# Ring slots of the expert tables' chunks: spacing of 4224 bytes in place of 4096

## The chip, the core and the metric

One core of a Trainium2 chip runs the whole kernel. The time is the device time of one execution in microseconds. TensorE multiplies, ScalarE, VectorE and GpSimd compute beside it, and SyncE issues most of the DMAs. All of them read and write one on-chip memory of 128 partitions; an address below is a byte offset inside a partition.

## What is computed

A decoder layer over 256 tokens of width 1024, in float32:

```
h = x + concat(norm(moba_attention(q_m, k_m, v_m)), norm(stick_breaking(q_s, k_s, v_s))) @ w_out
xn = rms_norm(h, ffn_norm)
# PEER: for each token 8 heads choose 16 experts each, of 128 * 128
hid = gelu(xn . u_table[expert])
h = h + sum over the chosen experts of gate * hid * v_table[expert]
h = h + sigmoid(rms_norm(h, ple_norm) @ w_gate) * (p @ w_ple)
```

The expert part is done densely. The kernel multiplies all 16384 rows of `u_table` with all tokens, multiplies the result by the gates (zero where an expert wasn't chosen), and multiplies that with all of `v_table`. Each table is 64 MB, read as 128 chunks of 128 experts, 512 KB each.

## The kernel before

**Precision.** A float32 operand is split in two parts of the matmul's own format, `hi` (a rounded copy) and `lo` (the rest), and each product is three matmuls: hi x hi, hi x lo, lo x hi. `three` (L1203 on) issues them: its first argument of a pair is the weights (stationary), the second the moving operand. So the weights run `ah, ah, al` and the moving operand `bh, bl, bh`.

**The ring.** A chunk of a table goes to one of `RING = 4` slots. `t_raw` holds the loaded float32 chunk, `t_hi` its rounded copy (ScalarE, `table_hi`, L583), and `t_lo` the rest (GpSimd at L1178 in the first pass, VectorE at L910 in the second), written in place of `t_raw`. Both tiles are `[P, RING, D]` with D = 1024, so the slots of each lie 4096 bytes apart. SyncE reloads a slot when TensorE is done with the chunk in it (`hid_done`, `v_used`), and ScalarE and the engine of `t_lo` work `LEAD = 2` chunks ahead of TensorE.

**The first pass** (L1440 on, some 190 to 583 us). For each chunk `hidden(q)` issues 24 matmuls: eight column blocks of 128 of `t_hi`, `t_hi`, `t_lo` as weights, and `xt_hi`, `xt_lo`, `xt_hi` (128 x 256, the normalised tokens) as moving operand. The result goes through Gelu into `slots`. From chunk 40 on (`late_step`) three of four chunks are followed by four matmuls of `gates` (L1481, weights `hot_i`, moving `hot_j`, 256 columns), which build the gates of four tokens.

**The second pass** (`expert_sum`, L1510 on, some 583 to 933 us). For each chunk 12 matmuls: weights `g_hi`, `g_hi`, `g_lo` (128 tokens each), moving operand `t_hi`, `t_lo`, `t_hi` (512 columns). They accumulate in four PSUM banks over all chunks.

**The other large products** have `xt_hi`, `xt_hi`, `xt_lo` as weights and 512 or 256 columns of `w_hi`, `w_lo` (or `wg_hi`, `wg_lo`) as moving operand (`rows_group`, `projection`, the end at L1563), or the reverse in `columns_group` (L1234). `embedding` has `pt_hi`, `pt_lo` as weights and `wp_hi`, `wp_lo` as moving operand.

**The addresses.** All tiles are placed by hand. `sizes` gives, in this order, `h` (8192 bytes), `xt_hi` (8192), `gains` (128), `xt_lo` (8192), `cst` (2048), `qkg` (128), `stats` (768), and then `ZONE` begins, with the ring and what goes with it. `BIG` begins behind that zone, with `w_raw`, `w_hi`, `w_lo`, `slots` and, 98304 bytes on, the tiles at `UP`.

Of the kernel before, what the change touches and what calls it, by code (L numbers as in the profile page):

```python
# [36 lines left out]
TOPK = 16  # L37
PH = 8
# [5 lines left out]
WARM = 3  # L44
RING = 4
LEAD = 2
FIRST = 40
EXP_AT = 32
PICKS_AT = 36
# [22 lines left out]
def layer_program(nc, x, x_t, p_t, rel_bias, bucket_onehot, consts, qk_gain, w_in, w_out, w_query,  # L72
# [5 lines left out]
    with ctx:  # L78
# [5 lines left out]
            where[name] = at  # L84
            at += 4 * n
        ZONE = at
        BIG = ZONE + 4 * 13312
        assert BIG + 4 * P * SEQ <= nc.sbuf_usable_end

        def tile(name, shape, offset, dt=f32):  # L90
# [28 lines left out]
        o = UP  # L119
# [41 lines left out]
        diag = tile("diag", [P, SEQ], ZONE + 4 * 10752)  # L161
        rstd_row = tile("rstd_row", [P, SEQ], ZONE + 4 * 11008)

        t_raw = tile("t_raw", [P, RING, D], ZONE)
        t_lo = tile("t_lo", [P, RING, D], ZONE, f32r)
        hit = tile("hit", [P, PH, TOPK, TOPK], ZONE + 4 * 4096)
        hot_i = tile("hot_i", [P, 2, 4, P], ZONE + 4 * 4096, f32r)
        hot_j = tile("hot_j", [P, 2, 4, 2, P], ZONE + 4 * 5120, f32r)
        g_hi = tile("g_hi", [P, RING, SEQ], ZONE + 4 * 4096, f32r)
        g_lo = tile("g_lo", [P, RING, SEQ], ZONE + 4 * 5120, f32r)  # L170
        t_hi = tile("t_hi", [P, RING, D], ZONE + 4 * 7168, f32r)
        o = ZONE + 4 * 11264
        pick_t = tile("pick_t", [P, 3, SEQ], o); o += 4 * 768
        sk = tile("sk", [P, 2, N_KEYS], o); o += 4 * 256
        pick = tile("pick", [P, TT, 2, P], o); o += 4 * 512
        gate = tile("gate", [P, TT, PH, TOPK], o); o += 4 * 256
        ratio = tile("ratio", [P, SEQ], o); o += 4 * 256
        assert o <= BIG
        low = tile("low", [P, 2, 4, P], ZONE + 4 * 12032)
        gate_hi = tile("gate_hi", [P, SEQ], ZONE + 4 * 12032, f32r)  # L180
        gate_lo = tile("gate_lo", [P, SEQ], ZONE + 4 * 12288)

        pairs = [ctx.enter_context(nc.psum_tensor(f"pair{k}", [P, 4, 2, P], f32)) for k in range(2)]
        bank = [pairs[b // 2][:, 2 * (b % 2):2 * (b % 2) + 2, :, :].rearrange("p a b c -> p (a b c)")
# [115 lines left out]
        @block.sync  # L300
        def _(sp):
            for c in range(2):
                sp.dma_start(w_raw[:, 0, c, :], w_in[0, :, c, :]).then_inc(piece_loaded[c], 16)
            for b in range(1, 4):
                cols = slice(4 * DC + 2 * SEQ * b, 4 * DC + 2 * SEQ * (b + 1))
                sp.dma_start(xt_raw[:, 2 * b:2 * b + 2, :].rearrange("p a b -> p (a b)"), x_t[:, cols]
                             ).then_inc(xt_loaded[b], 16)
                sp.dma_start(w_raw[:, 0, 2 * b:2 * b + 2, :], w_in[0, :, 2 * b:2 * b + 2, :]
                             ).then_inc(piece_loaded[b + 1], 16)
            for b in range(4):  # L310
                sp.dma_start(w_raw[:, 1, 2 * b:2 * b + 2, :], w_in[1, :, 2 * b:2 * b + 2, :]
                             ).then_inc(quarter_loaded[b], 16)
# [12 lines left out]
            sp.wait_ge(*split(0))
            for k in range(2):
                m = slice(256 * k, 256 * (k + 1))
                sp.dma_start(w_raw[:, 0, :, m], w_in[2, :, :, m]).then_inc(half_loaded[k], 16)
            for n in range(3, N_GROUPS):
                load_group(n)  # L330
                if n == 3:
                    sp.wait_ge(tab_copied, 1)
                    sp.dma_start(table.ap(), tab_out[:, :]).then_inc(tab_stored, 16)
                    sp.wait_ge(tab_stored, 16)
                    sp.dma_start(skew[:, :, :], bass.AP(table, 0, [[1, P], [TAB, NH], [1, SEQ]])
                                 ).then_inc(bias_loaded, 16)
                if n == 6:
                    sp.wait_ge(z_done, 2)
                    sp.dma_start(wp_raw[:, :, :], w_ple).then_inc(wp_loaded, 16)
                if n == 8:  # L340
                    sp.wait_ge(spv_out, 2)
                    sp.dma_start(pt_raw[:, :, :], p_t).then_inc(wp_loaded, 16)
                if n == 9:

                    sp.wait_ge(pv_out, 2)
                    sp.dma_start(sk[:, :, :], subkeys_t).then_inc(sk_loaded, 16)
                    for q in range(RING):
                        sp.dma_start(t_raw[:, q, :], u_chunks[q]).then_inc(t_loaded[q], 16)

            sp.wait_ge(ple_out, 4)  # L350
            sp.dma_start(ple_kept.ap(), ple[:, :, :]).then_inc(ple_stored, 16)

            def load_chunk(table, q, n):
                sp.dma_start(t_raw[:, q, :], table[bass.ds(n, 1)].rearrange("o p f -> (o p) f")
                             ).then_inc(t_loaded[q], 16)

            with sp.Fori(1, N_KEYS // RING) as i:
                for q in range(RING):
                    sp.wait_ge(hid_done, RING * i + q - RING + 1)
                    load_chunk(u_chunks, q, RING * i + q)  # L360
            for q in range(RING):
                sp.wait_ge(hid_done, N_KEYS - RING + q + 1)
                load_chunk(v_chunks, q, q)

            def v_loads(first, last, gate_weights):
                with sp.Fori(first, last) as i:
                    if gate_weights:
                        sp.dma_start(wg_raw[:, bass.ds(i - first, 1), :].rearrange("p o n -> p (o n)"),
                                     w_gate[:, bass.ds(i - first, 1), :].rearrange("p o n -> p (o n)")
                                     ).then_inc(wg_loaded, 16)  # L370
                    for q in range(RING):
                        sp.wait_ge(v_used, RING * i + q - RING + 1)
                        load_chunk(v_chunks, q, RING * i + q)

            v_loads(1, 12, False)
            sp.wait_ge(g_lo_ready, 32)
            v_loads(12, 20, True)
            sp.wait_ge(g_lo_ready, 72)
            sp.wait_ge(ple_stored, 16)
            sp.dma_start(ple_end[:, :, :], ple_kept.ap()).then_inc(ple_loaded, 16)  # L380
            v_loads(20, N_KEYS // RING, False)
            for u, (tt, d0, width, b) in enumerate(END_PARTS):
                sp.wait_ge(y_ready, u + 1)
                sp.dma_start(out[tt * P:(tt + 1) * P, d0:d0 + width], h[:, tt, d0:d0 + width]).then_inc(stored, 16)
            sp.wait_ge(stored, 16 * len(END_PARTS))
# [3 lines left out]
        def _(act):  # L389
# [190 lines left out]

            def table_hi(q, count):
                act.wait_ge(t_loaded[q % RING], 16 * count)
                nc.scalar.activation(t_hi[:, q % RING, :], t_raw[:, q % RING, :], ACT.Copy).then_inc(t_hi_ready, 1)  # L583

            for n in range(LEAD):
                table_hi(n, 1)
# [127 lines left out]
        def _(dve):  # L714
# [192 lines left out]

            def table_lo(q, count):
                dve.wait_ge(t_hi_ready, count)
                nc.vector.tensor_tensor(t_lo[:, q % RING, :], t_raw[:, q % RING, :],  # L910
                                        t_hi[:, q % RING, :].bitcast(f32), ALU.subtract).then_inc(t_lo_ready, 1)

            def top16(jobs):
                def each(op):
# [231 lines left out]
        def _(pool):  # L1146
# [28 lines left out]

            def table_lo(q, n):
                pool.wait_ge(t_hi_ready, n + 1)
                nc.gpsimd.tensor_tensor(t_lo[:, q, :], t_raw[:, q, :], t_hi[:, q, :].bitcast(f32),  # L1178
                                        ALU.subtract).then_inc(t_lo_pool, 1)

            for n in range(LEAD):
# [7 lines left out]
        def _(pe):  # L1189
# [250 lines left out]
            key_scores(3)  # L1440

            def hidden(q):
                three(hid_bank(q), [((t_hi[:, q, P * c:P * (c + 1)], t_lo[:, q, P * c:P * (c + 1)]),
                                               (xt_hi[:, c, :], xt_lo[:, c, :])) for c in range(DC)]
                      ).then_inc(hid_done, 1)

# [61 lines left out]
            def expert_sum(q, i, first=False, tiles=(0, 1)):  # L1508
# [6 lines left out]
                for tt in tiles:  # L1515
                    t = slice(P * tt, P * (tt + 1))
                    for w in range(2):
                        d = slice(512 * w, 512 * (w + 1))
                        dst = bank[2 * tt + w][:, :]
                        mm(dst, g_hi[:, q, t], t_hi[:, q, d], start=first and q == 0, stop=False,  # L1520
                           skip_group_check=True)
                        mm(dst, g_hi[:, q, t], t_lo[:, q, d], start=False, stop=False, skip_group_check=True)  # L1522
                        ins = mm(dst, g_lo[:, q, t], t_hi[:, q, d], start=False, stop=True,  # L1523
                                 skip_group_check=True)
                if 1 in tiles:
                    ins.then_inc(v_used, 1)
# [106 lines left out]
```

## Time and profile before

| | us |
|---|---|
| median of 3 runs | 962.65 (962.56 to 963.67) |
| the profiled execution | 962.73 |
| its span, first to last instruction | 961.0 |
| TensorE busy | 949.7 (99%) |
| VectorE / ScalarE / GpSimd busy | 692.4 / 610.5 / 331.6 |
| DMA, mean share of 16 engines; HBM | 52%; 179 GB/s |

Busy time of an engine is the time in which at least one of its instructions was under way. Matmuls are pipelined: the next one starts before the one before it has ended, so both the busy share and the length of a matmul say little on how fast they follow each other. That is read from their starts, in the timeline.

### The profile page before, as it was taken

How to read it: one execution, taken by the hardware profiler on the slowest of the kernel's cores; microseconds unless marked ns; L12 is line 12 of the kernel's file. 1: busy time of each engine (PE TensorE's matmuls, PEld its weight loads, DVE VectorE, ACT ScalarE, POOL GpSimd, SP SyncE). 2: the span in 40 equal slices, each digit the busy share in tenths (PEclk: the TensorE clock that was granted, in tenths of full speed). 3: DMA queues.
4: the chain of work that ended last, by engine and by line, in shares of the span. 5: the costliest groups of instructions: out<-in, count | busy, mean ns of one | idle time of the engine just before them, and what ended most of it. 6: DMA issues, size and time to landing. Idle time of an engine off the chain costs nothing.

```text
span 961.0 us, 19174 instructions
## 1 busy us (share of the span) xinstructions
PE 949.7 (99%) x6222; PEld 863.7 (90%) x6222; DVE 692.4 (72%) x1389; ACT 610.5 (64%) x1034; POOL 331.6 (35%) x148
## 2 busy tenths in 40 slices
PE   8999999999999999999999999999999999999998
PEld 5987889999999999999999998888888888888877
DVE  6747763999996888988888885555555555566763
ACT  7578664366676888888888885555445544556543
POOL 0002230178888777777777773000000000000000
PEclk9999999999999999999999999999999999999999
DMA  9770353045555544445454445555566666555521
GB/s 335 269 286 1 140 226 132 2 165 186 188 184 176 176 160 169 158 169 169 159 174 157 171 169 183 196 196 187 194 234 237 239 239 228 193 193 196 190 94 44
DMA packets 46459, 172.08 MB, mean 179 GB/s; under 512 B 5043, under 2 KB 8540, under 8 KB 44892
## 3 DMA queue, kind: packets, MB, share of 16 engines
q1 hardware_dynamic: 46284, 171.40, 52.0%
q8 instruction: 19, 0.31, 0.1%
q10 hardware_dynamic: 144, 0.28, 0.1%
q14 instruction: 12, 0.10, 0.0%
HBM read 169.55 MB, written 2.11 MB: 179 GB/s over the span
## 4 chain that ended last, share of the span: by engine, by line
PE 91%; DVE 4%; issue 2%; DMA 2%; ACT 1%; SPq 1%; POOL 1%; DVEq 0%; ACTq 0%; POOLq 0%
PE bank L1207 14%; PE bank L1206 14%; PE bank L1208 14%; PE pair L1520 12%; PE pair L1523 12%; PE pair L1522 12%; PE pair L1481 3%; PE pair L1236 1%; PE pair L1234 1%; PE pair L1235 1%; DMA w_raw<-w_in 1%; PE bank L1563 1%; PE bank L1236 1%; PE bank L1564 1%; PE bank L1565 1%
## 5 line engine op out<-in xcount | busy, mean ns | idle before, releaser
L583 ACT ACTIVATE t_hi<-t_raw 128x1024 fp32r<-128x1024 f32 x256 | 270.3, 1056 | 166.6 <-DMA t_raw<-v_chunks 162.6
L1178 POOL TENSOR_TENSOR t_lo<-t_raw,t_hi 128x1024 fp32r<-128x1024 f32 x130 | 311.5, 2409 | 144.0 <-ACT t_hi L583 143.9
L1207 PE MATMUL bank<-xt_lo,t_hi 128*128 128x256 f32 x1024 | 287.5, 281 | 0.0
L1206 PE MATMUL bank<-xt_hi,t_hi 128*128 128x256 f32 x1024 | 287.0, 280 | 0.2 <-POOL t_lo L1178 0.2
L1208 PE MATMUL bank<-xt_hi,t_lo 128*128 128x256 f32 x1024 | 286.5, 280 | 0.0
L910 DVE TENSOR_TENSOR t_lo<-t_raw,t_hi 128x1024 fp32r<-128x1024 f32 x126 | 154.4, 1225 | 136.7 <-ACT t_hi L583 136.5
L1520 PE MATMUL pair<-t_hi,g_hi 128*128 128x512 f32 x512 | 199.5, 390 | 0.1
L1522 PE MATMUL pair<-t_lo,g_hi 128*128 128x512 f32 x512 | 199.2, 389 | 0.0
L1523 PE MATMUL pair<-t_hi,g_lo 128*128 128x512 f32 x512 | 199.2, 389 | 0.0
L1208 PEld LDWEIGHTS bank<-xt_hi,t_lo 128*128 128x128 f32 x1024 | 193.1, 189 | 0.0
L1206 PEld LDWEIGHTS bank<-xt_hi,t_hi 128*128 128x128 f32 x1024 | 192.8, 188 | 0.4 <-POOL t_lo L1178 0.4
L1207 PEld LDWEIGHTS bank<-xt_lo,t_hi 128*128 128x128 f32 x1024 | 192.4, 188 | 0.0
L1520 PEld LDWEIGHTS pair<-t_hi,g_hi 128*128 128x128 f32 x512 | 96.1, 188 | 20.8 <-DVE g_lo L1090 1.1
L1523 PEld LDWEIGHTS pair<-t_hi,g_lo 128*128 128x128 f32 x512 | 96.1, 188 | 20.0
L1522 PEld LDWEIGHTS pair<-t_lo,g_hi 128*128 128x128 f32 x512 | 96.1, 188 | 19.9
L1043 DVE TENSOR_SCALAR hot_j<-bank,pick_t 128x128 fp32r<-128x128 f32 x256 | 86.9, 401 | 0.0
L634 ACT ACTIVATE hot_j<-hot_j,ratio 128x128 fp32r<-128x128 f32 x256 | 82.0, 394 | 0.0
L647 ACT ACTIVATE bank<-bank 128x256 f32<-128x256 f32 x88 | 32.4, 368 | 39.7 <-PE bank L1208 32.8
L1059 DVE TENSOR_TENSOR slots<-slots,bank 128x256 f32 (+1 forms) x88 | 36.3, 412 | 28.9 <-ACT bank L647 28.9
L1090 DVE TENSOR_TENSOR g_lo<-slots,g_hi 128x256 fp32r<-128x256 f32 x128 | 54.3, 424 | 0.6 <-ACT g_hi L657 0.6
L724 DVE TENSOR_TENSOR w_lo<-w_raw,w_hi 128x4096 fp32r<-128x4096 f32 x8 | 35.4, 4424 | 24.2 <-ACT w_hi L401 24.1
L657 ACT ACTIVATE g_hi<-slots 128x256 fp32r (+1 forms) x128 | 51.2, 400 | 0.6 <-DVE slots L1059 0.6
(270 smaller groups left out, 1293.8 us busy)
## 6 DMA issues: line engine op xcount, KB each, us to landing
t_raw<-u_chunks SPq DMA_DIRECT2D x128, 512.0 KB, 3.2
t_raw<-v_chunks SPq DMA_DIRECT2D x128, 512.0 KB, 3.3
w_raw<-w_query SPq DMA_DIRECT2D x4, 2048.0 KB, 7.6
w_raw<-w_in SPq DMA_DIRECT2D x3, 2048.0 KB, 10.9
w_raw<-w_out SPq DMA_DIRECT2D x2, 2048.0 KB, 8.3
wg_raw<-w_gate SPq DMA_DIRECT2D x8, 512.0 KB, 4.8
w_raw<-w_in SPq DMA_DIRECT2D x7, 512.0 KB, 8.4
w_raw<-w_in SPq DMA_DIRECT2D x2, 1024.0 KB, 10.3
```

What stands on the lines that cost most here:

```text
L583: nc.scalar.activation(t_hi[:, q % RING, :], t_raw[:, q % RING, :], ACT.Copy).then_inc(t_hi_ready, 1)
L634: ins = nc.scalar.activation(hot_j[:, k, q, 1, :], hot_j[:, k, q, 0, :].bitcast(f32), ACT.Copy, scale=ratio[:, bass.ds(4 * s + q, 1)])
L910: nc.vector.tensor_tensor(t_lo[:, q % RING, :], t_raw[:, q % RING, :], t_hi[:, q % RING, :].bitcast(f32), ALU.subtract).then_inc(t_lo_read ...
L1043: nc.vector.tensor_scalar(hot_j[:, k, q, 0, :], lanes, pick_t[:, 1, bass.ds(t, 1)], pick_t[:, 2, bass.ds(t, 1)], ALU.is_equal, ALU.mult).t ...
L1090: nc.vector.tensor_tensor(g_lo[:, k, :], src, g_hi[:, k, :].bitcast(f32), ALU.subtract).then_inc(g_lo_ready, 1)
L1178: nc.gpsimd.tensor_tensor(t_lo[:, q, :], t_raw[:, q, :], t_hi[:, q, :].bitcast(f32), ALU.subtract).then_inc(t_lo_pool, 1)
L1206: mm(dst, ah, bh, start=(c == 0), stop=False)
L1207: mm(dst, ah, bl, start=False, stop=False)
L1208: ins = mm(dst, al, bh, start=False, stop=(c == n - 1))
L1520: mm(dst, g_hi[:, q, t], t_hi[:, q, d], start=first and q == 0, stop=False, skip_group_check=True)
L1522: mm(dst, g_hi[:, q, t], t_lo[:, q, d], start=False, stop=False, skip_group_check=True)
L1523: ins = mm(dst, g_lo[:, q, t], t_hi[:, q, d], start=False, stop=True, skip_group_check=True)
```

## The change

Each slot of `t_raw`, `t_lo` and `t_hi` takes 1024 + 32 words in place of 1024, so that slots lie 4224 bytes apart; the 32 words between two slots are not used. The tiles become flat, and `ring_of` makes a list of four views of 1024 words. What follows in the zone moves: `hit`, `hot_i`, `hot_j`, `g_hi`, `g_lo` and `t_hi` by 96 words (384 bytes), `pick_t`, `sk`, `pick`, `gate`, `ratio`, `low`, `gate_hi`, `gate_lo` and `BIG` with all in it by 192 words (768 bytes). `xt_hi`, `xt_lo` and the start of `t_raw` stay, and `pt_hi`, `pt_lo` and the other tiles placed from `ZONE` do too. All instructions, their order and their waits are as before; the other edits of the diff write `t_hi[q]` for `t_hi[:, q, :]`.

```diff
+SLOT = D + 32
-        BIG = ZONE + 4 * 13312
+        BIG = ZONE + 4 * 13504
-        t_raw = tile("t_raw", [P, RING, D], ZONE)
-        t_lo = tile("t_lo", [P, RING, D], ZONE, f32r)
-        hit = tile("hit", [P, PH, TOPK, TOPK], ZONE + 4 * 4096)
-        hot_i = tile("hot_i", [P, 2, 4, P], ZONE + 4 * 4096, f32r)
-        hot_j = tile("hot_j", [P, 2, 4, 2, P], ZONE + 4 * 5120, f32r)
-        g_hi = tile("g_hi", [P, RING, SEQ], ZONE + 4 * 4096, f32r)
-        g_lo = tile("g_lo", [P, RING, SEQ], ZONE + 4 * 5120, f32r)
-        t_hi = tile("t_hi", [P, RING, D], ZONE + 4 * 7168, f32r)
-        o = ZONE + 4 * 11264
+        def ring_of(t):
+            return [t[:, SLOT * q:SLOT * q + D] for q in range(RING)]
+
+        t_raw = ring_of(tile("t_raw", [P, RING * SLOT - 32], ZONE))
+        t_lo = ring_of(tile("t_lo", [P, RING * SLOT - 32], ZONE, f32r))
+        hit = tile("hit", [P, PH, TOPK, TOPK], ZONE + 4 * 4192)
+        hot_i = tile("hot_i", [P, 2, 4, P], ZONE + 4 * 4192, f32r)
+        hot_j = tile("hot_j", [P, 2, 4, 2, P], ZONE + 4 * 5216, f32r)
+        g_hi = tile("g_hi", [P, RING, SEQ], ZONE + 4 * 4192, f32r)
+        g_lo = tile("g_lo", [P, RING, SEQ], ZONE + 4 * 5216, f32r)
+        t_hi = ring_of(tile("t_hi", [P, RING * SLOT - 32], ZONE + 4 * 7264, f32r))
+        o = ZONE + 4 * 11456
...
             def hidden(q):
-                three(hid_bank(q), [((t_hi[:, q, P * c:P * (c + 1)], t_lo[:, q, P * c:P * (c + 1)]),
+                three(hid_bank(q), [((t_hi[q][:, P * c:P * (c + 1)], t_lo[q][:, P * c:P * (c + 1)]),
```

## Rows read from the trace of the kernel before

**Rows 1.** The cores, then the page: busy time, and the chain that ended last.

```profile
core 0: 961.0 us, clock 0.999
...
PE 949.7 (99%) x6222; PEld 863.7 (90%) x6222; DVE 692.4 (72%) x1389; ACT 610.5 (64%) x1034; POOL 331.6 (35%) x148
...
PE 91%; DVE 4%; issue 2%; DMA 2%; ACT 1%; SPq 1%; POOL 1%; DVEq 0%; ACTq 0%; POOLq 0%
PE bank L1207 14%; PE bank L1206 14%; PE bank L1208 14%; PE pair L1520 12%; PE pair L1523 12%; PE pair L1522 12%; PE pair L1481 3%; PE pair L1236 1%; PE pair L1234 1%; PE pair L1235 1%; DMA w_raw<-w_in 1%; PE bank L1563 1%; PE bank L1236 1%; PE bank L1564 1%; PE bank L1565 1%
```

**Rows 2.** Longest wait of TensorE: us in total, times, longest.

```profile
PE bank L1241 <- DVE warm L749: 1.5, 1, 1.5
```

**Rows 3.** Groups of ScalarE and VectorE, ring first; then the chunk's DMA (KB, us).

```profile
L583 ACT ACTIVATE t_hi<-t_raw 128x1024 fp32r<-128x1024 f32 x256 | 270.3, 1056 | 166.6 <-DMA t_raw<-v_chunks 162.6
L910 DVE TENSOR_TENSOR t_lo<-t_raw,t_hi 128x1024 fp32r<-128x1024 f32 x126 | 154.4, 1225 | 136.7 <-ACT t_hi L583 136.5
...
L437 ACT ACTIVATE w_hi<-w_raw 128x1024 fp32r<-128x1024 f32 x4 | 4.2, 1062 | 0.8 <-DMA w_raw<-w_in 0.7
...
L761 DVE TENSOR_TENSOR w_lo<-w_raw,w_hi 128x1024 fp32r<-128x1024 f32 x4 | 4.9, 1224 | 0.1
...
t_raw<-v_chunks SPq DMA_DIRECT2D x128, 512.0 KB, 3.3
```

**Rows 4.** Timeline of TensorE (start us, us long): a chunk's first matmul, both passes.

```profile
242.15 0.28 PE L1206 MATMUL bank<-xt_hi,t_hi 128*128 128x256 f32 x1
244.98 0.28 PE L1206 MATMUL bank<-xt_hi,t_hi 128*128 128x256 f32 x1
253.46 0.28 PE L1206 MATMUL bank<-xt_hi,t_hi 128*128 128x256 f32 x1
...
719.22 0.39 PE L1520 MATMUL pair<-t_hi,g_hi 128*128 128x512 f32 x1
721.93 0.39 PE L1520 MATMUL pair<-t_hi,g_hi 128*128 128x512 f32 x1
730.10 0.39 PE L1520 MATMUL pair<-t_hi,g_hi 128*128 128x512 f32 x1
```

**Rows 5.** Timeline: second pass, 864 matmuls apart; embedding, three matmuls apart.

```profile
602.25 0.39 PE L1520 MATMUL pair<-t_hi,g_hi 128*128 128x512 f32 x1
...
798.10 0.39 PE L1520 MATMUL pair<-t_hi,g_hi 128*128 128x512 f32 x1
...
133.26 0.39 PE L1206 MATMUL pair<-wp_hi,pt_hi 128*128 128x512 f32 x1
...
133.94 0.39 PE L1206 MATMUL pair<-wp_hi,pt_hi 128*128 128x512 f32 x1
```

**Rows 6.** Timeline: input projection of V, 72 matmuls apart.

```profile
64.12 0.39 PE L1206 MATMUL bank<-w_hi,xt_hi 128*128 128x512 f32 x1
...
80.76 0.39 PE L1206 MATMUL bank<-w_hi,xt_hi 128*128 128x512 f32 x1
```

**Rows 7.** Timeline: the last gate product, 45 matmuls apart.

```profile
951.46 0.28 PE L1563 MATMUL bank<-wg_hi,xt_hi 128*128 128x256 f32 x1
...
956.82 0.28 PE L1563 MATMUL bank<-wg_hi,xt_hi 128*128 128x256 f32 x1
```

**Rows 8.** Timeline: first pass, 384 matmuls apart, then 48 apart.

```profile
225.19 0.28 PE L1206 MATMUL bank<-xt_hi,t_hi 128*128 128x256 f32 x1
...
270.42 0.28 PE L1206 MATMUL bank<-xt_hi,t_hi 128*128 128x256 f32 x1
...
299.31 0.28 PE L1206 MATMUL bank<-xt_hi,t_hi 128*128 128x256 f32 x1
...
304.91 0.28 PE L1206 MATMUL bank<-xt_hi,t_hi 128*128 128x256 f32 x1
```

**Rows 9.** Timeline: first matmul of the first pass and of the second.

```profile
190.73 0.36 PE L1206 MATMUL bank<-xt_hi,t_hi 128*128 128x256 f32 x1
...
583.17 0.39 PE L1520 MATMUL pair<-t_hi,g_hi 128*128 128x512 f32 x1
```

More of the change, by code:

```diff
@@ L178, in layer_program @@
         assert o <= BIG
-        low = tile("low", [P, 2, 4, P], ZONE + 4 * 12032)
-        gate_hi = tile("gate_hi", [P, SEQ], ZONE + 4 * 12032, f32r)
-        gate_lo = tile("gate_lo", [P, SEQ], ZONE + 4 * 12288)
+        low = tile("low", [P, 2, 4, P], ZONE + 4 * 12224)
+        gate_hi = tile("gate_hi", [P, SEQ], ZONE + 4 * 12224, f32r)
+        gate_lo = tile("gate_lo", [P, SEQ], ZONE + 4 * 12480)
         pairs = [ctx.enter_context(nc.psum_tensor(f"pair{k}", [P, 4, 2, P], f32)) for k in range(2)]
@@ L347, in _ @@
                     for q in range(RING):
-                        sp.dma_start(t_raw[:, q, :], u_chunks[q]).then_inc(t_loaded[q], 16)
+                        sp.dma_start(t_raw[q], u_chunks[q]).then_inc(t_loaded[q], 16)
             sp.wait_ge(ple_out, 4)
@@ L353, in load_chunk @@
             def load_chunk(table, q, n):
-                sp.dma_start(t_raw[:, q, :], table[bass.ds(n, 1)].rearrange("o p f -> (o p) f")
+                sp.dma_start(t_raw[q], table[bass.ds(n, 1)].rearrange("o p f -> (o p) f")
                              ).then_inc(t_loaded[q], 16)
@@ L582, in table_hi @@
                 act.wait_ge(t_loaded[q % RING], 16 * count)
-                nc.scalar.activation(t_hi[:, q % RING, :], t_raw[:, q % RING, :], ACT.Copy).then_inc(t_hi_ready, 1)
+                nc.scalar.activation(t_hi[q % RING], t_raw[q % RING], ACT.Copy).then_inc(t_hi_ready, 1)
             for n in range(LEAD):
@@ L909, in table_lo @@
                 dve.wait_ge(t_hi_ready, count)
-                nc.vector.tensor_tensor(t_lo[:, q % RING, :], t_raw[:, q % RING, :],
-                                        t_hi[:, q % RING, :].bitcast(f32), ALU.subtract).then_inc(t_lo_ready, 1)
+                nc.vector.tensor_tensor(t_lo[q % RING], t_raw[q % RING],
+                                        t_hi[q % RING].bitcast(f32), ALU.subtract).then_inc(t_lo_ready, 1)
             def top16(jobs):
@@ L1177, in table_lo @@
                 pool.wait_ge(t_hi_ready, n + 1)
-                nc.gpsimd.tensor_tensor(t_lo[:, q, :], t_raw[:, q, :], t_hi[:, q, :].bitcast(f32),
+                nc.gpsimd.tensor_tensor(t_lo[q], t_raw[q], t_hi[q].bitcast(f32),
                                         ALU.subtract).then_inc(t_lo_pool, 1)
@@ L1519, in expert_sum @@
                         dst = bank[2 * tt + w][:, :]
-                        mm(dst, g_hi[:, q, t], t_hi[:, q, d], start=first and q == 0, stop=False,
+                        mm(dst, g_hi[:, q, t], t_hi[q][:, d], start=first and q == 0, stop=False,
                            skip_group_check=True)
-                        mm(dst, g_hi[:, q, t], t_lo[:, q, d], start=False, stop=False, skip_group_check=True)
-                        ins = mm(dst, g_lo[:, q, t], t_hi[:, q, d], start=False, stop=True,
+                        mm(dst, g_hi[:, q, t], t_lo[q][:, d], start=False, stop=False, skip_group_check=True)
+                        ins = mm(dst, g_lo[:, q, t], t_hi[q][:, d], start=False, stop=True,
                                  skip_group_check=True)
```

## Prediction, made before the changed kernel was run

> **What bounds the kernel now.** I read the page first: the span is 961.0 us and TensorE is busy 949.7 us of it, at a mean granted clock of 0.999 of full speed (the 2.4 GHz level) [rows 1]. The chain of work that ended last is 91% TensorE, and six matmul lines hold 78% of it: L1206 to L1208, the first table's products, 14% each, and L1520, L1522, L1523, the second table's, 12% each [rows 1]. Then the waits of TensorE: ten kinds, of which the longest is 1.5 us [rows 2]. The large waits, ScalarE's 162.6 us for the chunks' DMA and VectorE's 136.5 us for `t_hi` [rows 3], lie ahead of engines with room. In the second pass a chunk's DMA takes 3.3 us, its `t_hi` 1.06 us and its `t_lo` 1.23 us, 5.6 us together, while a chunk takes TensorE 2.72 us [rows 4] and the load goes out three chunks (8.2 us) before TensorE wants the chunk. So 2.6 us are to spare, and no time of a DMA, of ScalarE or of VectorE decides anything short of that. What decides is TensorE's pitch, the time from one matmul's start to the next one's start. A busy share of 99% does not show it, because a 128x512 matmul is 389 ns long and starts 227 ns after the one before.
>
> **The change part by part.** No instruction, DMA, wait or semaphore is added, removed or moved, and the lengths stay: that part costs 0. What moves is addresses inside a partition. Take them as remainders modulo 512 bytes, measured from `xt_hi`. Before, every tile that TensorE reads in the two table passes is at 0, except `xt_lo`, which is at 128 (it follows `gains`, 4*8*4 = 128 bytes). After, `t_lo` of slot q is at 128q, `t_hi` of slot q at 384+128q (the tile moved by 96 words, 384 bytes), `g_hi`, `g_lo`, `hot_i` and `hot_j` at 384, and all that hangs on `BIG` (`w_hi`, `w_lo`, `wp_hi`, `wg_hi`, `wg_lo`) at 256. `hi` and `lo` of one slot thus lie 128 bytes apart (modulo 512) where they were aligned.
>
> The engines that fill the ring first. `t_hi` takes 1056 ns in the ring and 1062 ns for the same width out of `w_raw`; `t_lo` takes VectorE 1225 ns in the ring and 1224 ns for the same width outside [rows 3]. A ring that suffered from its 4096-byte spacing would show more than its neighbours. Nothing to win there: 0, under the cover of the 2.6 us.
>
> Is TensorE slowed by what the others write into the ring? In the first pass a chunk begins at 242.15, the next at 244.98 and the fourth after the first at 253.46: 2.83 us for the one slot and 11.31 / 4 = 2.83 over all four. In the second, at 719.22, 721.93 and 730.10: 2.71 and 10.88 / 4 = 2.72 us. They are the same while DMA, ScalarE and VectorE come and go [rows 4]. So the slots do not collide with each other, and spacing them brings nothing by itself. The Trainium skill states the same more strongly ("SBUF — State Buffer", section "Who interferes with whom": only the port pair of VectorE and GpSimd is contended; TensorE waits on nobody); the trace agrees. By that page alone the sum of the whole change would be 0, which is rival 1.
>
> But TensorE's own two streams, the weight load of the next matmul and the moving operand of the present one, do show a pattern that follows the addresses:
> - 128x512, weights `g_hi, g_hi, g_lo` (all at 0): 864 matmuls from 602.25 to 798.10, 226.7 ns each [rows 5]. The embedding's, with `pt_hi, pt_hi, pt_lo` (all at 0), have settled to the same: 133.26 to 133.94 is three, 227 ns each [rows 5].
> - 128x512, weights `xt_hi, xt_hi, xt_lo` (0, 0, 128): 72 matmuls from 64.12 to 80.76, 231.1 ns each [rows 6]: 226.7 and twice 233.
> - 128x256, weights `xt_hi, xt_hi, xt_lo` (0, 0, 128), in the end: 45 from 951.46 to 956.82, 119.1 ns [rows 7].
> - 128x256 in the first pass, weights `t_hi, t_hi, t_lo` (all at 0), moving operand `xt_hi, xt_lo, xt_hi` (0, 128, 0): 384 from 225.19 to 270.42, 117.8 ns, and 48 from 299.31 to 304.91, 116.7 ns [rows 8]. Two rhythms occur with the same addresses, and which one comes is set when the flow is disturbed.
> So weights that alternate by 128 bytes go with a longer pitch at both widths, and a moving operand that alternates by 128 bytes does not. After the change the first pass's weights are at 384+128q, 384+128q, 128q: they alternate by 128.
>
> First pass: from 190.73 to 583.17 it takes 392.4 us [rows 9], for 3072 matmuls of the table and the 256 of `gates`, of the same width: 392.4 / 3328 = 117.9 ns. At 119.1 ns instead: 3072 x 1.2 ns = 3.7 us; against the longer rhythm's 117.8 it is 3072 x 1.3 = 4.0. I take 4.0. Its bounds: if all chunks fell into the short rhythm, 3072 x -1.1 = -3.4 us; if each paid the 4.4 ns that 128x512 shows, +13.6 us. The nearest row is the one of the same width, hence 4.0.
> Second pass: weights all at 384, no alternation; only the moving operand alternates, and it stands off the weights by 128q or 128q+128. The first pass shows this free. Taken at 0; bounds: 1536 x 4.4 ns = +6.8 us if it pays as [rows 6] do; below, the pitch of 226.7 ns is 13 ns over the 213 ns that 512 columns need at the 2.4 GHz level, so if an offset removed half of it, 1536 x -6.7 = -10 us.
> Weights and moving operands of the first 190 us and of the end: weights alternate as before; only the distance of 256 between `xt` and `w` is new. Some 360 wide matmuls x up to 6.7 ns either way = -2.4 to +2.4 us, taken at 0.
> Sum: 961.0 + 4.0 = 965.0 us of span. The profiled execution took 962.7 us, 1.7 outside the span and equal to the median of 962.65: 966.7 us.
>
> **The rivals.**
> 1. The low address bits do not matter. For it: the slots' equality [rows 4], and that the stages of [rows 5] and [rows 6] also differ in where their tiles lie altogether. Against it: the embedding reads weights and `wp_hi` as far apart as the input stage does and has the short pitch. Time: 962.7, give or take 0.7 for the rhythms of the first pass.
> 2. The second pass pays too, because what counts is that the moving operand stands off the weights being loaded, which `t_hi` against `g_hi` then does in most slots: +6.8 on the sum, 973.5 us. Against it: the 256-wide first pass has such a moving operand in each third matmul and no cost. For it: only at 512 is the weight load short beside the stream, so the first pass may hide it. It decides from 1 ns a matmul (1.5 us).
> 3. Faster: the 13 ns above 213 are themselves a meeting of the two streams at equal addresses, and an offset parts them; or the first pass falls into its short rhythm throughout (959.3). For it: the pitch is not one fixed number even now. Price with half of the 13 ns gone in the second pass: 952 to 957 us. Against: the only offset rows there are go the other way. A rule of the Trainium skill bears on its size ("TensorE: Matmul & The Clock Gate", section "Back-to-back issue gap": N/2.4 + 2.5 ns): it would give 215.8 ns at 512 columns; the trace shows 226.7 here, so an estimate from that page of what could be won is 17 us in the second pass.
>
> **How the numbers follow.** Forecast (first pass alone pays) 0.37; rival 2, 0.21; rival 1, 0.24; rival 3, 0.18. Predicted: 966.7 us. The range takes in rivals 1 and 2 and the short rhythm of rival 3: 958.5 to 975.0, leaving out the larger gains and the +13.6 us bound. This kernel's time can be told from no change at about 0.2% (1.9 us). Faster by more than that: rival 3, 0.17. Within: rival 1, 0.25. Slower: forecast and rival 2, 0.58.
>
> **What would show it.** Right: the starts of neighbouring chunks in the first pass 2.86 us apart or more instead of 2.80 to 2.83, TensorE's waits unchanged, chunks of the second pass still 2.72 us apart. The second pass at 2.77 speaks for rival 2, at 2.65 or less for rival 3; a pitch that differs between the four slots would show that the offset between the streams counts, not the alternation. All as before: rival 1. I would be wrong in kind if the change of time lay in waits, in `t_lo` or in the DMAs.

## The result

The changed kernel takes 970.49 us (median of 20 runs, 969.68 to 977.99) against 962.98 us (median of 20 runs) before: a ratio of 1.0078, with a 95% interval of 1.0067 to 1.0089. It is slower by 7.5 us. In some executions of several of these kernels the granted clock averaged 0.990 to 0.993 over the span, where it is otherwise 0.998 to 1.0, and they took some 6 to 9 us longer; the 977.99 is one. The profiled execution took 970.19 us, its span is 968.5 us.

Rows from the page of the changed kernel and, last, one from its list of waits. Lines of the source have moved by four: L1210 to L1212 are the first pass, L1524, L1526 and L1527 the second, L587 and L914 the ring's `hi` and `lo`.

```profile
PE 955.9 (99%) x6222; PEld 865.3 (89%) x6222; DVE 692.4 (71%) x1389; ACT 610.3 (63%) x1034; POOL 331.1 (34%) x148
...
L587 ACT ACTIVATE t_hi<-t_raw 128x1024 fp32r<-128x1024 f32 x256 | 270.2, 1056 | 172.8 <-DMA t_raw<-v_chunks 167.5
...
L914 DVE TENSOR_TENSOR t_lo<-t_raw,t_hi 128x1024 fp32r<-128x1024 f32 x126 | 154.4, 1225 | 141.8 <-ACT t_hi L587 141.4
L1524 PE MATMUL pair<-t_hi,g_hi 128*128 128x512 f32 x512 | 201.5, 394 | 0.0
L1527 PE MATMUL pair<-t_hi,g_lo 128*128 128x512 f32 x512 | 200.8, 392 | 0.0
...
PE bank L1245 <- DVE warm L753: 1.5, 1, 1.5
```

VectorE and ScalarE do the same work in the same time: 1056 and 1225 ns an instruction, as in [rows 3]. They idle 5 to 6 us longer; a slot is loaded again only when TensorE is done with it, and TensorE is slower. TensorE's longest wait is still the 1.5 us of [rows 2] (last line). One other wait grew, that for `w_lo` ahead of the first pass, from 0.2 to 1.5 us. Only TensorE's own busy time has grown, by 6.2 us, and its 512-wide matmuls are 392 to 394 ns long where they were 389 to 390.

Where the time went is read from the starts of the stages. The timeline of TensorE (start us, us long): the first matmul of the first pass, that of the second, and the last of the second in the changed kernel; then the last of the second pass in the kernel before.

```profile
191.27 0.36 PE L1210 MATMUL bank<-xt_hi,t_hi 128*128 128x256 f32 x1
...
585.24 0.40 PE L1524 MATMUL pair<-t_hi,g_hi 128*128 128x512 f32 x1
...
940.25 0.40 PE L1527 MATMUL pair<-t_hi,g_lo 128*128 128x512 f32 x1
```

```profile
932.78 0.39 PE L1523 MATMUL pair<-t_hi,g_lo 128*128 128x512 f32 x1
```

With [rows 9], stage by stage:

| us | before | after | difference |
|---|---|---|---|
| up to the first pass | 190.73 | 191.27 | +0.5 |
| first pass | 392.44 | 393.97 | +1.5 |
| second pass | 349.61 | 355.01 | +5.4 |
| from there to the end | 28.2 | 28.2 | 0.0 |

And within a pass, from the first matmuls of chunks: in the first pass two of slot 0, with three chunks between them, in the second pass five neighbours (slots 0, 1, 2, 3 and 0 again):

```profile
248.44 0.28 PE L1210 MATMUL bank<-xt_hi,t_hi 128*128 128x256 f32 x1
...
259.77 0.28 PE L1210 MATMUL bank<-xt_hi,t_hi 128*128 128x256 f32 x1
...
640.61 0.40 PE L1524 MATMUL pair<-t_hi,g_hi 128*128 128x512 f32 x1
643.40 0.39 PE L1524 MATMUL pair<-t_hi,g_hi 128*128 128x512 f32 x1
646.17 0.39 PE L1524 MATMUL pair<-t_hi,g_hi 128*128 128x512 f32 x1
648.94 0.39 PE L1524 MATMUL pair<-t_hi,g_hi 128*128 128x512 f32 x1
651.68 0.40 PE L1524 MATMUL pair<-t_hi,g_hi 128*128 128x512 f32 x1
```

In [rows 4] every chunk took 2.83 us in the first pass and 2.72 in the second, whatever its slot. The first pass still does on the mean, (259.77 - 248.44) / 4 = 2.83. The second takes 2.79, 2.77, 2.77 and 2.74 us in slots 0 to 3. So it stays for the first 79 chunks. Chunk 80 (counted from 0, as all chunks here) takes 2.80, and then to the end of the pass, again slots 0 to 3 and 0:

```profile
828.90 0.39 PE L1524 MATMUL pair<-t_hi,g_hi 128*128 128x512 f32 x1
831.67 0.39 PE L1524 MATMUL pair<-t_hi,g_hi 128*128 128x512 f32 x1
834.41 0.40 PE L1524 MATMUL pair<-t_hi,g_hi 128*128 128x512 f32 x1
837.20 0.39 PE L1524 MATMUL pair<-t_hi,g_hi 128*128 128x512 f32 x1
839.97 0.39 PE L1524 MATMUL pair<-t_hi,g_hi 128*128 128x512 f32 x1
```

Now slot 0 takes 2.77, slot 1 2.74, slot 2 2.79 and slot 3 2.77 us: slots 0 and 2 have changed places, and so have 1 and 3. So the addresses lengthen the chunks, but the four values are a rhythm of four chunks, which one disturbance shifts by two, and not each a property of its slot. (2.79 + 2.77 + 2.77 + 2.74) / 4 - 2.72 = 0.048 us, times 128 chunks, is 6.1 us. The stage grew by 5.4: in the kernel before six chunks had taken longer than 2.72 us, 0.8 us together, and here hardly one falls out of the rhythm.

### The profile page after: what moved, and what is told of

Read it like the earlier page. It is cut to its first block, busy times and chain, and to the rows that moved or that the text cites. A ratio compares the mean times of both kernels' runs of the same rounds, so it can differ in the third digit from the quotient of the medians.

```text
span 968.5 us, 19174 instructions
## 1 busy us (share of the span) xinstructions
PE 955.9 (99%) x6222; PEld 865.3 (89%) x6222; DVE 692.4 (71%) x1389; ACT 610.3 (63%) x1034; POOL 331.1 (34%) x148
## 4 chain that ended last, share of the span: by engine, by line
PE 92%; DVE 4%; issue 2%; DMA 1%; SPq 1%; POOL 1%; ACT 1%; POOLq 0%; DVEq 0%
PE bank L1211 14%; PE bank L1210 14%; PE bank L1212 14%; PE pair L1524 12%; PE pair L1527 12%; PE pair L1526 12%; PE pair L1485 3%; PE pair L1240 1%; PE pair L1238 1%; PE pair L1239 1%; DMA w_raw<-w_in 1%; PE bank L1567 1%; PE bank L1240 1%; PE bank L1569 1%; PE bank L1568 1%
## 5 line engine op out<-in xcount | busy, mean ns | idle before, releaser
L587 ACT ACTIVATE t_hi<-t_raw 128x1024 fp32r<-128x1024 f32 x256 | 270.2, 1056 | 172.8 <-DMA t_raw<-v_chunks 167.5
L1210 PE MATMUL bank<-xt_hi,t_hi 128*128 128x256 f32 x1024 | 287.2, 281 | 0.2 <-POOL t_lo L1182 0.2
L1212 PE MATMUL bank<-xt_hi,t_lo 128*128 128x256 f32 x1024 | 286.9, 280 | 0.0
L914 DVE TENSOR_TENSOR t_lo<-t_raw,t_hi 128x1024 fp32r<-128x1024 f32 x126 | 154.4, 1225 | 141.8 <-ACT t_hi L587 141.4
L1524 PE MATMUL pair<-t_hi,g_hi 128*128 128x512 f32 x512 | 201.5, 394 | 0.0
L1527 PE MATMUL pair<-t_hi,g_lo 128*128 128x512 f32 x512 | 200.8, 392 | 0.0
L1526 PE MATMUL pair<-t_lo,g_hi 128*128 128x512 f32 x512 | 200.8, 392 | 0.0
L1210 PEld LDWEIGHTS bank<-xt_hi,t_hi 128*128 128x128 f32 x1024 | 193.2, 189 | 0.4 <-POOL t_lo L1182 0.4
L1212 PEld LDWEIGHTS bank<-xt_hi,t_lo 128*128 128x128 f32 x1024 | 192.6, 188 | 0.0
L1527 PEld LDWEIGHTS pair<-t_hi,g_lo 128*128 128x128 f32 x512 | 96.1, 188 | 22.3
L1524 PEld LDWEIGHTS pair<-t_hi,g_hi 128*128 128x128 f32 x512 | 96.1, 188 | 21.9 <-DVE g_lo L1094 0.2
L1526 PEld LDWEIGHTS pair<-t_lo,g_hi 128*128 128x128 f32 x512 | 96.2, 188 | 21.7
```

The source lines that it names most:

```text
L587: nc.scalar.activation(t_hi[q % RING], t_raw[q % RING], ACT.Copy).then_inc(t_hi_ready, 1)
L914: nc.vector.tensor_tensor(t_lo[q % RING], t_raw[q % RING], t_hi[q % RING].bitcast(f32), ALU.subtract).then_inc(t_lo_ready, 1)
L1210: mm(dst, ah, bh, start=(c == 0), stop=False)
L1212: ins = mm(dst, al, bh, start=False, stop=(c == n - 1))
L1524: mm(dst, g_hi[:, q, t], t_hi[q][:, d], start=first and q == 0, stop=False, skip_group_check=True)
L1526: mm(dst, g_hi[:, q, t], t_lo[q][:, d], start=False, stop=False, skip_group_check=True)
```

## The experiments

Three theories stood. **A1**: it costs when `hi` and `lo` alternate by 128 bytes, as [rows 6] suggested. **A2**: it costs when the weights being loaded and the moving operand being read stand at different addresses, modulo some period. (Distance, below, is the address of the weights less that of the moving operand.) **B**: spacing the slots, or moving the tiles, costs by itself, through what the other engines write. Each chunk time below is the difference of the first matmuls' starts in the timeline.

**Alternation without spacing.** The changed kernel with the slots 4096 bytes apart again:

```diff
-SLOT = D + 32
+SLOT = D
...
```

> The changed kernel with its slots 4096 bytes apart again: the tiles stay moved (hot_i, hot_j, g_hi, g_lo, t_hi by 384 bytes, BIG by 768), so in all four slots t_hi is at 384 and t_lo at 0 (modulo 512), with the weights g at 384. This is what slot 0 of the changed kernel has. Theory A (the distance between the addresses of TensorE's two streams decides): every slot takes what slot 0 takes in the changed kernel, 2.79 us a chunk in the second pass and 2.84 in the first; 962.9 + 128 x 0.07 + 128 x 0.017 = about 974 us. Theory B (only the spacing of the slots matters, against what other engines write): 2.72 and 2.83 us a chunk again, about 963 us.

970.28 us (ratio 1.0069, 1.0043 to 1.0094). Two chunks of slot 0 in the second pass, with slots 1, 2 and 3 between them:

```profile
750.95 0.40 PE L1524 MATMUL pair<-t_hi,g_hi 128*128 128x512 f32 x1
...
762.04 0.40 PE L1524 MATMUL pair<-t_hi,g_hi 128*128 128x512 f32 x1
```

The whole loss is there with the old spacing, which speaks against B. The four chunks take 11.09 us, and each of them 2.77, 231.0 ns a matmul. That is the pitch of [rows 6], 231.1: one operand in three off by 128 bytes costs the same, whether it is a weight, as there, or a moving operand, as `t_lo` here. At 512 columns too a second rhythm occurs at the same addresses: after a disturbance the ten chunks from 820.56 to 848.56 us take 2.80 us each. The size missed: I had expected slot 0's 2.79 us everywhere, and 974 us.

**Spacing without alternation.** The changed kernel with the four places of `t_hi` handed out in another order, so that `hi` and `lo` of a slot have equal remainders:

```diff
         t_hi = ring_of(tile("t_hi", [P, RING * SLOT - 32], ZONE + 4 * 7264, f32r))
+        t_hi = t_hi[1:] + t_hi[:1]
```

> The changed kernel with slot q of t_hi put at place q+1 (slot 3 at place 0) of the same tile: slots stay 4224 bytes apart, but hi and lo of one slot have the same remainder modulo 512, 128q. Theory A1 (what costs is that hi and lo alternate by 128 bytes): the cost goes, 2.72 us a chunk in the second pass in every slot, 963 to 964 us. Theory A2 (what costs is a standing distance between weights and moving operand): only slot 3, where t is at 384 like g, takes 2.72 us; the others stay at 2.74 to 2.79 us, 968 to 971 us. Theory B (the spacing itself): as the changed kernel, 970.5 us.

970.72 us (1.0074, 1.0049 to 1.0099):

```profile
752.26 0.40 PE L1525 MATMUL pair<-t_hi,g_hi 128*128 128x512 f32 x1
755.05 0.39 PE L1525 MATMUL pair<-t_hi,g_hi 128*128 128x512 f32 x1
757.79 0.40 PE L1525 MATMUL pair<-t_hi,g_hi 128*128 128x512 f32 x1
760.58 0.39 PE L1525 MATMUL pair<-t_hi,g_hi 128*128 128x512 f32 x1
763.32 0.40 PE L1525 MATMUL pair<-t_hi,g_hi 128*128 128x512 f32 x1
```

2.79, 2.74, 2.79, 2.74 us. Nothing alternates inside a slot, so A1 alone is out. The moving operand stands at 0, 128, 256, 384 and the weights at 384. At distances of 0 and 256 the chunk is nearly at its old time, at 128 and 384 it is dear: the distance counts, and 256 bytes are as good as none.

The first pass of the same trace answers A1 once more. Here `t_hi` and `t_lo` of a slot, its weights, do not alternate, and yet the pass is longer than the changed kernel's 393.97 us, by 1.7 us:

```profile
190.77 0.36 PE L1211 MATMUL bank<-xt_hi,t_hi 128*128 128x256 f32 x1
...
586.40 0.40 PE L1525 MATMUL pair<-t_hi,g_hi 128*128 128x512 f32 x1
```

**Distances in steps of 64 bytes.** The kernel before, with slot q of `g_hi` and `g_lo` moved by 64q bytes, then by 256 + 64q:

```diff
+        G_OFF = (0, 16, 32, 48)
...
+        g_hi = [g_hi_t[:, SEQ * q + G_OFF[q]:SEQ * (q + 1) + G_OFF[q]] for q in range(RING)]
...
```

> The kernel before with slot q of g_hi and of g_lo moved by 64q bytes, both alike: in the second pass nothing alternates, and the weights stand 0, 64, 128 or 192 bytes off the moving operand. Theory A1 (alternation): all slots 2.72 us a chunk, 963.0 us. Theory A2 (standing distance): slot 0 2.72 us, slot 2 (128 bytes) dearer by 0.02 to 0.07 us, and slots 1 and 3 tell whether 64 bytes matter; a slot under 2.72 us would mean that equal addresses are not the best. Theory B: all 2.72 us.

> The kernel before with slot q of g_hi and g_lo moved by 256 + 64q bytes. Theory A2 with a period of 256 bytes (which the two-slot pattern of e2_halves_aligned says: 2.735 us at distances 256 and 0, 2.792 at 128 and 384): slot by slot the same chunk times as e4_g_offsets, 2.73, 2.80, 2.79, 2.75 us. With a period of 512: different ones, slot 0 above 2.74 us.

968.4 us and, in a single run, 968.11 us. The second pass of the first of them, slots 0, 1, 2, 3 and 0:

```profile
749.39 0.39 PE L1523 MATMUL pair<-t_hi,g_hi 128*128 128x512 f32 x1
752.12 0.40 PE L1523 MATMUL pair<-t_hi,g_hi 128*128 128x512 f32 x1
754.91 0.39 PE L1523 MATMUL pair<-t_hi,g_hi 128*128 128x512 f32 x1
757.71 0.39 PE L1523 MATMUL pair<-t_hi,g_hi 128*128 128x512 f32 x1
760.46 0.39 PE L1523 MATMUL pair<-t_hi,g_hi 128*128 128x512 f32 x1
```

2.73, 2.79, 2.80 and 2.75 us; in the second of them 2.73, 2.80, 2.79 and 2.75. A2 holds with a period of 256 bytes, and no distance tried at 512 columns is better than 0.

**Wider spacing, remainders kept.** The changed kernel with the slots of `t_raw` and `t_lo` 4096 + 256 bytes apart and all else a multiple of 256 away from its old place:

```diff
-SLOT = D + 32
+SLOT = D + 64
...
-        t_hi = ring_of(tile("t_hi", [P, RING * SLOT - 32], ZONE + 4 * 7264, f32r))
+        t_hi = ring_of(tile("t_hi", [P, RING * D], ZONE + 4 * 7360, f32r), D)
...
```

> The changed kernel with the slots of t_raw and t_lo 4096 + 256 bytes apart, those of t_hi 4096, and the tiles behind moved by 768 bytes: the slots are spaced still wider than in the changed kernel, but every remainder modulo 256 is that of the kernel before. Theory A2 with a period of 256: all as before, 2.72 and 2.80 to 2.83 us a chunk, 963.0 us. Theory B (the spacing, or moving the tiles, costs by itself): slower by several us, as the changed kernel. Period of 512: slots 1 and 3 dearer.

962.74 us (1.0003, 0.9994 to 1.0013). The profiled execution is one of 968.91 us, but its extra time lies ahead of the first pass, which begins at 197.18 us; in the passes the chunks take 2.83 and 2.72 us, as before, but for a few that a disturbance meets. This rules B out: the slots of `t_raw` and `t_lo` can be spaced more widely than in the change, and `t_hi` moved, at no cost and no gain, as long as the remainders stay.

**The first pass, all aligned.** The kernel before with 224 words moved ahead of `gains`, so that `xt_lo` has the remainder of all the rest:

```diff
-        sizes = dict(h=2 * D, xt_hi=DC * SEQ, gains=4 * DC, xt_lo=DC * SEQ, cst=4 * P, qkg=32, stats=192)
+        sizes = dict(h=2 * D, xt_hi=DC * SEQ, qkg=32, stats=192, gains=4 * DC, xt_lo=DC * SEQ, cst=4 * P)
```

> The kernel before with qkg and stats placed ahead of gains, so that xt_lo has the same remainder modulo 512 as xt_hi and as all else; nothing more. Theory A in either form: the 512-wide products with xt as weights go from 231.1 to 226.7 ns (360 matmuls x 4.4 ns = 1.6 us), the 256-wide ones at the end from 119.1 to below 118 ns; for the first pass, whose moving operand no longer alternates, no row tells, between -3 and +1 us. Sum 958 to 962.5 us. Theory B: no change, 963.0 us, 231.1 ns.

971.13 us (1.008, 1.0054 to 1.0105). First two rows the input projection, 78 matmuls apart; then four chunks of the first pass:

```profile
64.01 0.39 PE L1206 MATMUL bank<-w_hi,xt_hi 128*128 128x512 f32 x1
...
81.69 0.39 PE L1206 MATMUL bank<-w_hi,xt_hi 128*128 128x512 f32 x1
...
261.81 0.28 PE L1206 MATMUL bank<-xt_hi,t_hi 128*128 128x256 f32 x1
...
273.33 0.28 PE L1206 MATMUL bank<-xt_hi,t_hi 128*128 128x256 f32 x1
```

At 512 columns A2 is right: 17.68 / 78 = 226.7 ns, down from 231.1 in [rows 6]. At 256 columns the sign turns, which I had not expected: 11.52 / 96 = 120.0 ns, where [rows 8] have 116.7 and 117.8. The gate product at the end, for which I had expected less than 118 ns, went up as well, from 119.1 to 119.8. Equal addresses are the best at 512 columns and the worst tried at 256. The 128 bytes of `gains` ahead of `xt_lo` had been worth 8 us.

**Both passes by slot.** Slot q of all ring tiles and of `g_hi`, `g_lo` moved by 64q bytes, so that the second pass keeps distance 0 and the first gets 0, 64, 128, 192; first with `xt_lo` aligned, then with it in its old place:

```diff
+        OFF = (0, 16, 32, 48)
...
+        def ring_of(t, n):
+            return [t[:, n * q + OFF[q]:n * (q + 1) + OFF[q]] for q in range(RING)]
...
```

> The kernel of e3_xt_aligned (xt_lo aligned with xt_hi, so that nothing alternates) with slot q of t_raw, t_lo, t_hi, g_hi and g_lo moved by 64q bytes, all alike, and hot_i, hot_j kept aligned. In the first pass the weights t stand 0, 64, 128 or 192 bytes off the moving operand xt; in the second pass t and g are at equal remainders. Theory A2 (distance of the two streams, modulo 256): second pass 2.72 us in all slots; first pass 2.88 us in slot 0 as in e3_xt_aligned, and other values in the rest, which tell which distance is best at 256 columns. If equal addresses are the worst at this width, slots 1 to 3 lie below 2.88, and below the 2.83 of before if alternation was only part of the gain. A theory by absolute address would move the second pass too.

> The same 64-byte steps of the slots as in e6_slots64_xt_aligned, but with xt_lo where it was before, 128 bytes off xt_hi. Theory A2: second pass 2.72 us in all slots; first pass slot 0 as before, 2.80 to 2.83 us, slot 2 (distances 128, 0, 128 in place of 0, 128, 0) near it, slots 1 and 3 anywhere between 2.75 and 2.88. Total 958 to 970 us.

968.77 us and 969.78 us. The first of them, five chunks of the first pass, one later chunk of slot 3 with the start of the next, and two of the second pass:

```profile
260.39 0.28 PE L1211 MATMUL bank<-xt_hi,t_hi 128*128 128x256 f32 x1
263.28 0.28 PE L1211 MATMUL bank<-xt_hi,t_hi 128*128 128x256 f32 x1
266.01 0.28 PE L1211 MATMUL bank<-xt_hi,t_hi 128*128 128x256 f32 x1
268.84 0.28 PE L1211 MATMUL bank<-xt_hi,t_hi 128*128 128x256 f32 x1
271.67 0.28 PE L1211 MATMUL bank<-xt_hi,t_hi 128*128 128x256 f32 x1
...
367.06 0.28 PE L1211 MATMUL bank<-xt_hi,t_hi 128*128 128x256 f32 x1
369.78 0.28 PE L1211 MATMUL bank<-xt_hi,t_hi 128*128 128x256 f32 x1
...
750.65 0.39 PE L1525 MATMUL pair<-t_hi,g_hi 128*128 128x512 f32 x1
753.41 0.39 PE L1525 MATMUL pair<-t_hi,g_hi 128*128 128x512 f32 x1
```

2.89, 2.73, 2.83, 2.83 us in slots 0 to 3; later on slot 3 takes 2.72, and slot 1 has gone over to 117.8 ns a matmul. So at 256 columns distances of 64 and 192 bytes can give 113.3 ns, and they can give 117.8. In the other kernel, with `xt_lo` in its old place, a chunk of the first pass, up to the gates, takes 2.82 to 2.83 us in slots 0 and 1, 2.84 to 2.86 in slot 2 and 2.80 to 2.83 in slot 3, near what I had expected.

The second pass missed in both kernels: 2.76 us in nearly every chunk though its distance is 0. It is not the place that costs: `e9_xt_aligned_64`, below, has both operands at 64 in the second pass, and 2.72 us. Here both streams step by 64 bytes from one chunk to the next, and after each step ten of a chunk's twelve matmuls are irregular, 224 to 236 ns apart, before the pitch is back at 226 to 227 ns. A2 was too simple: a change of the addresses costs too, until the flow has settled again. At each step the first weights of the next chunk are loaded beside the last moving operand of the present one, 64 bytes off it; whether that one meeting makes the cost, or the step itself, no run separates.

**One distance for the whole first pass.** The aligned kernel with unused words ahead of `ZONE`: 16, 48 and 8 words, 64, 192 and 32 bytes:

```diff
-        sizes = dict(h=2 * D, xt_hi=DC * SEQ, qkg=32, stats=192, gains=4 * DC, xt_lo=DC * SEQ, cst=4 * P)
+        sizes = dict(h=2 * D, xt_hi=DC * SEQ, qkg=32, stats=192, gains=4 * DC, xt_lo=DC * SEQ, cst=4 * P, pad=16)
```

> The kernel of e3_xt_aligned (xt_lo aligned with xt_hi) with 64 unused bytes ahead of ZONE: everything from the ring on stands 64 bytes off xt, the ring, g, hot, w and the rest stay aligned with each other. In the first pass every weight stands 64 bytes ahead of the moving operand, as in slot 1 of e6_slots64_xt_aligned, which there had 113.7 ns a matmul before the gates began and 117.9 after. Theory A2 (the distance of the two streams decides): between 3072 x (117.9 - 120.2) and 3072 x (113.4 - 120.2) against e3_xt_aligned, 950 to 964 us in all, the second pass 2.72 us a chunk; the 512-wide products with xt as weights stand at 192, which e4_g_offsets showed at 229 ns. Theory C (only alternation or absolute places matter): as e3_xt_aligned, 971 us.

> The same with 192 unused bytes: in the first pass every weight stands 192 bytes ahead, as in slot 3 of e6_slots64_xt_aligned, which there had 117.9 ns before the gates began and 113.3 after. Theory A2: 950 to 964 us in all, second pass 2.72 us a chunk, the 512-wide products with xt as weights at 233 ns. Theory C: 971 us.

> The kernel of e9_xt_aligned_64 with 32 unused bytes ahead of ZONE in place of 64: weights and moving operand of the first pass stand 32 bytes apart. If only whole steps of 64 bytes count, this is a distance of 0, 120.0 ns in the first pass and 971 us, as e3_xt_aligned. If each 4-byte column counts, something between the pitches at 0 and at 64, 113.3 to 120 ns, 950 to 968 us.

With 64 bytes 954.98 us (0.9921, 0.9905 to 0.9937), 16 us better than with 0 and 7.5 us better than the kernel before. With 192 bytes 960.31 us, not told from before by the interval (0.9999, 0.9977 to 1.0021); but three of its 11 executions are of the longer kind named with the result, and the other eight, 959.29 to 961.23, all lie below the 17 of the kernel before, 962.01 to 963.57. With 32 bytes 966.11 us (1.0041, 1.0027 to 1.0054) and about 118.3 ns in the first pass, so steps below 64 bytes count as well. In all three kernels the tiles of the second pass lie 64, 192 or 32 bytes from where they were, at distance 0, and its chunks take 2.72 us: what counts is the distance, not the place. The 512-wide products ahead of the first pass have `xt` as weights, so that the same padding gives them the distance the other way round. With 64 bytes (distance 192) they take 229.0 ns, with 192 bytes (distance 64) 233.3 ns, as expected from `e4_g_offsets`, and with 32 bytes (distance 224) 233.3 ns too. The 64-byte kernel: one early chunk; then, later, chunks with the gate matmuls (L1481) between them.

```profile
200.69 0.28 PE L1206 MATMUL bank<-xt_hi,t_hi 128*128 128x256 f32 x1
...
203.41 0.28 PE L1206 MATMUL bank<-xt_hi,t_hi 128*128 128x256 f32 x1
...
306.26 0.28 PE L1206 MATMUL bank<-xt_hi,t_hi 128*128 128x256 f32 x1
...
309.00 0.63 PE L1481 MATMUL pair<-hot_j,hot_i 128*128 128x256 f32 x4
309.47 0.28 PE L1206 MATMUL bank<-xt_hi,t_hi 128*128 128x256 f32 x1
...
312.30 0.64 PE L1481 MATMUL pair<-hot_j,hot_i 128*128 128x256 f32 x4
```

2.72 us for the early chunk; later 309.00 - 306.26 = 2.74 and 312.30 - 309.47 = 2.83. There are two steady rhythms at this distance, 113.3 and 117.8 ns, and in this trace each group of gate matmuls turns one into the other. Between the early chunk and the gates it is 117.8 throughout: in chunk 8 one matmul starts 219 ns after the one before it, and the short rhythm of chunks 3 to 7 doesn't come back. In this trace, of the slowest of the six executions (958.18 us), 48 of the 128 chunks have the short rhythm.

**The gates at the same distance.** The same kernel with `hot_j` moved, so that all weights of the first pass stand at 64 and all moving operands at 0, the gates' too:

```diff
...
-        hot_j = tile("hot_j", [P, 2, 4, 2, P], ZONE + 4 * 5120, f32r)
+        hot_j = tile("hot_j", [P, 2, 4, 2, P], ZONE + 4 * 5168, f32r)
...
-        t_hi = tile("t_hi", [P, RING, D], ZONE + 4 * 7168, f32r)
+        t_hi = tile("t_hi", [P, RING, D], ZONE + 4 * 7232, f32r)
...
```

> The kernel of e9_xt_aligned_64 with hot_j moved by 192 bytes and t_hi and what lies behind it by 256: now in the first pass all weights (t_hi, t_lo, hot_i) are 64 bytes past a multiple of 256 and all moving operands (xt_hi, xt_lo, hot_j) at 0, while in e9_xt_aligned_64 the four gate matmuls between two chunks had both at 64. There the pitch of the first pass had two rhythms, 113.3 and 117.8 ns, and each group of gate matmuls turned one into the other. If the step of the distance at the gates is what turns it (theory A2 with a memory), the rhythm now stays over the gates: 113.3 ns all along from the first chunk that has it, the gates at 113.3 too, the first pass shorter by up to 60 x 0.107 + 256 x 0.0045 = 7.6 us, 948 to 951 us in all; or 117.8 all along, 960 us. If the gates turn it for another reason, as e9_xt_aligned_64, 955 us.

959.69 us (0.9961, 0.994 to 0.9982): between the two times expected, and spread from 952.94 to 964.04 in 12 runs (to 962.06 without one of the longer kind). In the profiled execution (955.48 us, span 953.8):

```profile
336.28 0.28 PE L1206 MATMUL bank<-xt_hi,t_hi 128*128 128x256 f32 x1
339.00 0.62 PE L1481 MATMUL pair<-hot_j,hot_i 128*128 128x256 f32 x4
339.46 0.29 PE L1206 MATMUL bank<-xt_hi,t_hi 128*128 128x256 f32 x1
342.29 0.64 PE L1481 MATMUL pair<-hot_j,hot_i 128*128 128x256 f32 x4
```

From the fourth chunk up to 339.00 the chunks take 2.72 us, over the gates too; from 339.46 on they take 2.83 to the end of the pass, without a wait that the trace shows. The rhythm does stay over the gates now, as the theory had it, but so does the bad one once it is there. And what turns it isn't simple: here too one matmul of chunk 8 starts late, after 221 ns, and the short rhythm goes on. By estimate that can make up to 128 x 0.107 = 13.7 us between executions; 9 us were seen. Again 48 of the 128 chunks have the short rhythm, so the two traces don't show why the version with the turning gates is the better one. By its median it is: **955 us, the fastest kernel of this study**.

## Why the prediction came out as it did

The time (970.5 for 966.7) and its sign were right and in the range; the split of it was not, and that the total came so near is in part luck: the forecast put all of the loss in the pass that gave a fifth of it, and nothing in the pass that gave most.
- **What bounds, and what doesn't.** Right. It was TensorE's pitch that moved, and not the ring's engines or the DMA. That spacing brings nothing by itself was right too (`e8_slots256`), and so was the reading that the low address bits of TensorE's two operands set the pitch, taken from [rows 5] against [rows 6]. (The embedding was a thin row for it: only one of its two groups of twelve settles to 227 ns, the other stays between 224 and 236.) Rival 1 is out.
- **First pass, +4.0 forecast, +1.5 measured.** The pass did grow, but not by the mechanism forecast, weights that alternate by 128 bytes. In `e2_halves_aligned` the weights of a slot don't alternate, and the pass grows by 3.2 us (395.63 for 392.44). The distances between the two operands decide. The term was also too large: its price came from [rows 7], 119.1 ns, a stage where only the weights alternate; here the moving operand alternates as well, and the mean pitch of the table's matmuls became 118.1 ns where it had been 117.7.
- **Second pass, 0 forecast, +5.4 measured.** This is the step that failed: "The first pass shows this free". It carried a row of 256 columns over to 512. `e3_xt_aligned` shows that at 256 columns the offset moving operand is better than free (120.0 ns without it), while `e1_shift_only` shows that at 512 it costs 4.4 ns a matmul. That is rival 2, which had been given 0.21, and the prediction's own sign of it came, chunks of 2.77 us in the second pass. Its reason (only at 512 is the weight load short beside the stream) is still only argued; its price, 4.4 ns x 1536 = 6.8 us, was close to the 6.1 us of undisturbed chunks.
- **The rest, 0 forecast, +0.5 measured**, inside its bounds of 2.4 us. The new distance of 256 between `xt` and `w` did nothing: the 512-wide products take 231.1 ns as before. `e1_shift_only` and `e2_halves_aligned`, with the same tiles in the same places up to there, begin the first pass at 190.82 and 190.77 us, so the 0.5 us isn't shown to come from the change.
- **Rival 3** was wrong for the change and right in kind. At distance 0 the pitch is 226.7 ns at 512 columns and 120.0 at 256, so the second 256 columns take 106.7 ns. If the first 256 take as long, 13.3 ns come on top at either width (an estimate from these two rows). Part of these 13.3 ns is a matter of placement. It is to be had in the first pass, not in the second, at 64 bytes, where 113.3 ns leave half of it: `e9_xt_aligned_64`.

## What to carry to other kernels

Where TensorE is the bound and busy at 99%, read the pitch from the starts of its matmuls, chunk by chunk: here a pitch that differed by stage or by slot at one shape came from where weights and moving operand lay, or from which of two rhythms had set in, not from work. Treat moving any tile as a change of TensorE's time: keep the remainders modulo 256 bytes of both operands when tiles are moved for other reasons, and measure the distance between them (0, 32, 64, 128, 192) for each width, since the best at 512 columns was the worst tried at 256. Profile more than one execution where two rhythms occur. And don't move a price found at one width to another.

## What the runs showed of the hardware

- The time of a chunk repeats to 1 ns over dozens of chunks, while the other engines come and go, and depends on the distance between the address of the weights and that of the moving operand, modulo 256 bytes. At 512 columns a chunk of 12 matmuls takes 2.72 us at a uniform distance of 0, and, in a kernel whose slots step through the distances, 2.80 at 64, 2.79 at 128 and 2.75 at 192; at 224 bytes the pitch is 233.3 ns, where 0 has 226.7. At 256 columns: 120.0 ns at 0, 118.3 at 32 and at 128, and 113.3 or 117.8 at 64 and 192; in the gate product at the end 116.7 at 224 (`e12_xt_aligned_32`).
- The Trainium skill ("SBUF — State Buffer", section "Who interferes with whom") has it that TensorE waits on nobody. The runs agree as to where the other engines write (`e8_slots256`, 962.74 us), and differ as to TensorE itself: its pitch is not independent of how the addresses of its two operands lie (226.7 to 233.3 ns at 512 columns). The measurement decides here.
- Two rhythms can stand at the same addresses, and a disturbance, or a group of other matmuls, picks one; where both operands step by 64 bytes from chunk to chunk, at distance 0 within each, a chunk takes 2.76 us for 2.72.
- What inside the chip makes the streams meet is open. So is why the changed kernel's second pass has a rhythm of four chunks, though modulo 256 its addresses repeat every two, and what turned the rhythm at 339 us in the last kernel.
